# Hybrid decoder step: four buffers for the experts' down weights instead of two, and the last gate rows read at the end

## The reference

```python
scores = sigmoid(xf @ w_router); idx = top 8 of 64 (by groups); w = normalised scores of these * 2.5
def _swiglu(x, wg, wu, wd):              # per expert: wg, wu (1024 x 256), wd (256 x 1024)
    return (silu(x @ wg) * (x @ wu)) @ wd
f = sum over the 8 experts of w * _swiglu(row) + shared expert
x = x + g2 * rms_norm(f, norm_post_ffn)  # g2: the last gate, one row for the prompt, one per sample sequence
```

## Time and profile before

| | us |
|---|---|
| median of 3 runs | 1226.64 (1225.98 to 1227.47) |
| the profiled execution | 1225.67 |
| its span, first to last instruction | 1223.5 |
| TensorE busy | 1106.1 (90%) |
| VectorE busy | 903.4 (74%) |
| ScalarE busy | 642.7 (53%) |
| HBM read and written | 317.00 MB and 42.86 MB |

### The profile page before, as it was taken

How to read it: one execution, slowest core, us unless ns; L and a number is a source line. 1 busy time by engine, 2 the same in 40 slices (tenths; PEclk the granted TensorE clock), 3 DMA queues, 4 the chain that set the end, 5 groups by cost and what they waited for, 6 DMA issues and landing times.

```text
span 1223.5 us, 18540 instructions
## 1 busy us (share of the span) xinstructions
PE 1106.1 (90%) x6014; PEld 811.6 (66%) x6014; DVE 903.4 (74%) x1333; ACT 642.7 (53%) x770; POOL 181.9 (15%) x185
## 2 busy tenths in 40 slices
PE   5999999999989999799999999999999999999700
PEld 3899999865444454467777777777777777777500
DVE  4422443365956777579899999989989888888878
ACT  4332221332421233257787777777777777777501
POOL 1000000000110110112222222222222222221102
PEclk9999999998879999899999999999999999999855
DMA  9542221436974143689999999999999999998996
GB/s 341 188 133 80 80 80 40 157 98 202 315 276 132 44 138 120 235 325 381 380 388 391 391 384 385 387 387 381 373 381 383 373 381 379 375 375 314 352 360 210
DMA packets 86545, 339.34 MB, mean 277 GB/s; under 512 B 12561, under 2 KB 36129, under 8 KB 59122
## 3 DMA queue, kind: packets, MB, share of 16 engines
q1 hardware_dynamic: 70130, 301.16, 67.2%
q0 software_dynamic: 16384, 37.78, 8.8%
HBM read 317.00 MB, written 42.86 MB: 294 GB/s over the span
## 4 chain that ended last, share of the span: by engine, by line
PE 46%; DMA 32%; DVE 14%; ACT 6%; issue 2%; SPq 1%; DVEq 0%; POOL 0%; POOLq 0%; ACTq 0%
DMA arena<-in_w_exp_down 28%; PE ps L1828 11%; DVE down_lo L1648 4%; PE ps L2259 4%; PE ps L2067 4%; ACT down_hi L1120 4%; PE ps L2238 3%; PE ps L2239 3%; PE ps L2240 3%; PE ps L1821 2%; PE ps L2242 1%; PE ps L2105 1%; PE ps L2226 1%; DMA arena<-expert_rows 1%; PE ps L2140 1%
## 5 line engine op out<-in xcount | busy, mean ns | idle before, releaser
L1653 DVE TENSOR_TENSOR gu_lo<-w_gu,gu_hi 128x2048 fp32r<-128x2048 f32 (+1 forms) x128 | 258.7, 2022 | 6.4 <-ACT gu_hi L1114 1.1
L1114 ACT ACTIVATE gu_hi<-w_gu 128x2048 fp32r<-128x2048 f32 (+1 forms) x128 | 217.9, 1703 | 0.0
L1648 DVE TENSOR_TENSOR down_lo<-arena,down_hi 128x2048 fp32r<-128x2048 f32 x64 | 146.7, 2293 | 58.0 <-ACT down_hi L1120 58.0
L2238 PE MATMUL ps<-gu_hi,xT_hi 128*112 128x512 f32 x448 | 182.8, 408 | 3.3 <-DVE xT_lo L1658 2.2
L2239 PE MATMUL ps<-gu_lo,xT_hi 128*112 128x512 f32 x448 | 177.9, 397 | 0.0
L2240 PE MATMUL ps<-gu_hi,xT_lo 128*112 128x512 f32 x448 | 177.3, 396 | 0.0
L1120 ACT ACTIVATE down_hi<-arena 128x2048 fp32r<-128x2048 f32 x64 | 122.7, 1918 | 64.0 <-DMA arena<-in_w_exp_down 56.1
L814 POOL DMA_INDIRECT expert_rows<-arena,row_idx x64 | 69.1, 1079 | 356.2 <-ACT arena L1159 340.1
L2259 PE MATMUL ps<-down_hi,actT_hi 128*112 128x512 f32 x256 | 106.6, 416 | 5.5 <-DVE actT_lo L1643 5.5
L807 POOL DMA_INDIRECT arena<-h_rows,token_idx x64 | 80.6, 1259 | 203.1 <-PE ps L2226 156.1
L1828 PE MATMUL ps<-w_hi,hT_hi 128*128 128x300 f32 x352 | 105.6, 300 | 1.4 <-DVE w_lo L1231 1.4
(11 more groups left out here) (310 smaller groups left out, 1989.8 us busy)
## 6 DMA issues: line engine op xcount, KB each, us to landing
w_gu<-in_w_exp_gate SPq DMA_DIRECT2D x64, 1024.0 KB
w_gu<-in_w_exp_up SPq DMA_DIRECT2D x64, 1024.0 KB
arena<-in_w_exp_down SPq DMA_DIRECT2D x64, 1024.0 KB
arena<-in_w_ada SPq DMA_DIRECT2D x16, 1024.0 KB, 6.9
arena<-in_w_in SPq DMA_DIRECT2D x12, 1200.0 KB, 5.6
arena<-expert_rows SPq DMA_DIRECT2D x9, 1024.0 KB, 13.4
arena<-in_w_ada_first SPq DMA_DIRECT2D x4, 2048.0 KB, 16.2
arena<-expert_rows SPq DMA_DIRECT2D x4, 2048.0 KB, 13.0
```

Source lines behind the costliest of these rows:

```text
L1114: a.activation(gu_hi[b % RING][:, :, ks], w_gu[b % U][:, :, ks], ACT.Copy).then_inc(s_ghi, 1)
L1648: v.tensor_tensor(down_lo[:, :, :], w_dn[b % RING], down_hi[:, :, :].bitcast(F32), ALU.subtract).then_inc(s_dlo, 1)
L1653: v.tensor_tensor(gu_lo[b % U][:, :, ks], w_gu[b % U][:, :, ks], gu_hi[b % RING][:, :, ks].bitcast(F32), ALU.subtract).then_inc(s_glo, 1)
L2238: pe.matmul(out, x_hi, gu_hi[r][:, :, k], start=(k == 0), stop=False)
```

## The change

The raw down weights get four buffers, one per block of a turn, and `load_down` is issued four blocks ahead, right behind `load_gate_up` of the same block. The two new buffers are not contiguous: each row of 8 KB is laid in two pieces of 4 KB, 20 KB apart or more, in gaps of the arena (`apart`). To free these gaps, `x_raw`, `onehot`, `tab`, `bcg2` and a few sums move to other offsets. Down loads of blocks 2 and 3 are now issued ahead of the loop in place of the gate rows, which are read after it: the 0.5 MB read first of all, the eight small ones behind the third `ranks_low` read. No down load is left after the loop. Two semaphores of the front part are used again, with a base of 32 to the count. ScalarE loses one wait (for the x1 store) ahead of its first `x_high`.

```diff
-        x_raw = region(PROJ0 + 4 * D, 2, KT - SPLIT, T)
-        HB0 = XT0 + 4 * SPLIT * T
+        x_raw = region(XT0 + 4 * SPLIT * T, 2, KT - SPLIT, T)
+        HB0 = XT0 + 4 * KT * T
...
-        w_dn = [region(a + W_COLS[0], FK, D) for a in RING_AT]
+        def apart(first, second):
+            return arena[:, first:first + 2 * (second - first)].rearrange("p (k n) -> p k n", k=FK)[:, :, 0:D]
+
+        DN3 = (ARENA_W - 2 * (ARENA_W - WORK0 - 10 * D), WORK0 + 10 * D)
+        w_dn = [region(a + W_COLS[0], FK, D) for a in RING_AT] + [apart(PROJ0 + 4 * D, PROJ0 + 9 * D), apart(*DN3)]
...
-        s_wdn = [sem(f"w_down_in{r}") for r in range(RING)]
+        s_wdn = [sem(f"w_down_in{r}") for r in range(RING)] + [s_cond, s_const]
+        WDN_BASE = (0, 0, 32, 32)
...
-                    sp.wait_ge(s_dlo, j - RING + 1)
+                    sp.wait_ge(s_dlo, j - U + 1)
...
-                sp.dma_start(w_dn[b % RING], down).then_inc(s_wdn[b % RING], 16)
+                sp.dma_start(w_dn[b], down).then_inc(s_wdn[b], 16)
...
             load_gate_up(3, 3, False)
-            sp.dma_start(bcg2[0]...)                       # 0.5 MB
-            for b in range(SB): sp.dma_start(bcg2[1]...)   # 8 x 32 KB
+            load_down(2, 2, False)
+            load_down(3, 3, False)
             last = last_turn(sp)
             with sp.Fori(0, last) as i:
                 for b in range(U):
                     load_gate_up(i * U + (U + b), b, True)
-                    load_down(i * U + (b + RING), (b + RING) % U, True)
+                    load_down(i * U + (U + b), b, True)
...
-            load_down(last * U + RING, RING, True)
+            sp.wait_ge(s_dlo, last * U + 1)
+            sp.dma_start(bcg2[0]...)
             sp.wait_ge(s_free, last * U + 2)
             for t in range(2):
                 sp.wait_ge(s_gu, last * U + (t + 1))
                 rank_rows(ranks_low[t], 0, 4, t)
-            load_down(last * U + 3, 3, True)
             for t in range(2, NT):
...
                 rank_rows(ranks_low[t], 0, 4, t)
+                if t == 2:
+                    for b in range(SB): sp.dma_start(bcg2[1]...)
             sp.wait_ge(s_gu, last * U + 4)
+            sp.wait_ge(s_dlo, last * U + 3)
             for rows, buf in kept(N, shared): ...
             sp.wait_ge(s_free, last * U + 4)
-            sp.wait_ge(s_dlo, last * U + 3)
...  (ScalarE)
-                a.wait_ge(s_wdn[b % RING], 16 * (turns * 2 + (b % U // RING - 1)))
+                a.wait_ge(s_wdn[b % U], WDN_BASE[b % U] + 16 * turns)
...
-            a.wait_ge(s_mst, 32 + 32)
             x_high(0, 0)
```

More of the change, by code:

```diff
@@ L106 @@
 W_COLS = (2 * KT * FF, FK * D)
+GU_HI0, GU_HI1 = WORK0 + W_COLS[0] + W_COLS[1], HT0 + D // 2
+assert GU_HI0 + 2 * KT * FF == WORK0 + 10 * D and GU_HI1 + 2 * KT * FF <= ST0
 def _constants():
@@ L202, in hybrid_step @@
         actT_lo = over_arena("actT_lo", MOD0 + 2 * FK * D + 2 * FK * T, [P, 2, FK, T])
-        gu_hi = [over_arena(f"gu_hi{n}", at, [P, 2, SPLIT, FF]) for n, at in enumerate((WORK0 + W_COLS[0] + W_COLS[1], HT0))]
+        gu_hi = [over_arena(f"gu_hi{n}", at, [P, 2, SPLIT, FF]) for n, at in enumerate((GU_HI0, GU_HI1))]
         gu_lo = [over_arena(f"gu_lo{n}", at, [P, 2, KT, FF]) for n, at in enumerate(GU_AT)]
@@ L207, in hybrid_step @@
         pos_tab = over_arena("pos_tab", POS0, [P, MAXC * ECOL * NT], BF16)
-        OH0 = POS0 + MAXC * ECOL * NT // 2
+        OH0 = _consts["selp"][0]
+        TAB0 = _consts["chunk"][0] + 10 - 4 * P
         onehot = over_arena("onehot", OH0, [P, 2, NT, T], BF16)
-        XT0 = (OH0 + NT * T + 15) // 16 * 16
+        assert OH0 + NT * T <= TAB0 and TAB0 >= _consts["before"][0] + P and TAB0 + 4 * P <= _consts["dret"][0]
+        XT0 = (POS0 + MAXC * ECOL * NT // 2 + 15) // 16 * 16
         xT_hi = over_arena("xT_hi", XT0, [P, 2, SPLIT, T])
@@ L332, in hybrid_step @@
         rowf = small(5, P, rows=1)
-        tab = region(_consts["before"][0] + P, 4, P, rows=1).bitcast(I32)
+        tab = region(TAB0, 4, P, rows=1).bitcast(I32)
         act_rows = region(MOD0 + 2 * FK * D + 4 * FK * T, 2, FF)
         silu_g = region(MOD0 + 2 * FK * D + 4 * FK * T + 2 * FF, 2, FF)
-        w_dn = [region(a + W_COLS[0], FK, D) for a in RING_AT]
+        def apart(first, second):
+            return arena[:, first:first + 2 * (second - first)].rearrange("p (k n) -> p k n", k=FK)[:, :, 0:D]
+        DN3 = (ARENA_W - 2 * (ARENA_W - WORK0 - 10 * D), WORK0 + 10 * D)
+        w_dn = [region(a + W_COLS[0], FK, D) for a in RING_AT] + [apart(PROJ0 + 4 * D, PROJ0 + 9 * D), apart(*DN3)]
+        assert DN3[0] >= HB0 + 2 * D and DN3[0] + D <= WORK0 and DN3[1] + D == GU_HI1
         x_rows = region(HB0, 2, D)
@@ L353, in hybrid_step @@
         ranks_low = [region(GU_AT[t % 3 if t < 3 else t - 3], 4, D) for t in range(NT)]
-        ranks_mid = [region(a, 2, D) for a in (ST0 + D, WORK0 + D, WORK0 + W_COLS[0] + W_COLS[1], HT0, WORK0 + W_COLS[0])]
+        ranks_mid = [region(a, 2, D) for a in (ST0 + D, WORK0 + D, GU_HI0, GU_HI1, GU_HI1 + 2 * D)]
         ranks_high = [region(a, 2, D) for a in (ST0 + W_COLS[0], MOD0, MOD0 + 2 * D, _consts["dret"][0], HB0)]
-        ffn_sum = [region(a, D) for a in (HB0 + 2 * D, POS0, _consts["dret_s"][0], WORK0, ST0)]
-        assert HB0 + 3 * D <= WORK0 and POS0 + D <= XT0
+        ffn_sum = [region(a, D) for a in (WORK0 + W_COLS[0], POS0, _consts["dret_s"][0], WORK0, ST0)]
+        assert MAXC * ECOL * NT // 2 <= D
         sq2 = region(WORK0 + 8 * D, D)
-        bcg2 = [region(WORK0 + W_COLS[0] + W_COLS[1] + 2 * SPLIT * FF, D), region(HT0 + 2 * SPLIT * FF, D)]
-        assert WORK0 + W_COLS[0] + W_COLS[1] + 2 * SPLIT * FF + D <= HT0 and HT0 + 2 * SPLIT * FF + D <= ST0
+        bcg2 = [region(WORK0 + W_COLS[0] + D, D), region(GU_HI0 + 3 * D, D)]
         ps = ctx.enter_context(nc.psum_tensor("ps", [P, 8, 512], F32))
         xT_ps = ps[:, 4:6, :].rearrange("p b (q n) -> p (b q) n", n=XQ)[:, :, 0:T]
-        s_const = sem("consts_in")
-        s_cond = sem("cond_in")
+        s_const = sem("consts_and_fourth_down_in")
+        s_cond = sem("cond_and_third_down_in")
         s_rows = sem("rows_first_sample_rows_and_gla_state_in")
@@ L728, in rank_rows @@
                 sp.dma_start(to[0:ROWS[t], 0:k], by_rank[t * P:t * P + ROWS[t], first:first + k]).then_inc(s_yb[t], 16)
-            load_down(last * U + RING, RING, True)
+            sp.wait_ge(s_dlo, last * U + 1)
+            sp.dma_start(bcg2[0].rearrange("p (c n) -> p c n", n=512), mod_row[1, 0:1, 2:4].broadcast_to([P, 2, 512])).then_inc(s_bcg, 16)
             sp.wait_ge(s_free, last * U + 2)
@@ L741, in _ @@
                 rank_rows(ranks_low[t], 0, 4, t)
+                if t == 2:
+                    for b in range(SB):
+                        sp.dma_start(bcg2[1][b * SS:(b + 1) * SS].rearrange("p (c n) -> p c n", n=512),
+                                     mod_row[1, 1 + b:2 + b, 2:4].broadcast_to([SS, 2, 512])).then_inc(s_bcg, 16)
             sp.wait_ge(s_gu, last * U + 4)
+            sp.wait_ge(s_dlo, last * U + 3)
             for rows, buf in kept(N, shared):
@@ L1116, in down_high @@
             def down_high(j, b, turns):
-                a.wait_ge(s_wdn[b % RING], 16 * (turns * 2 + (b % U // RING - 1)))
+                a.wait_ge(s_wdn[b % U], WDN_BASE[b % U] + 16 * turns)
                 if not (isinstance(j, int) and j < 1):
                     a.wait_ge(s_y, j)
-                a.activation(down_hi[:, :, :], w_dn[b % RING], ACT.Copy).then_inc(s_dhi, 1)
+                a.activation(down_hi[:, :, :], w_dn[b % U], ACT.Copy).then_inc(s_dhi, 1)
             gate_up_high(0, 0, 0, 1)
@@ L1647, in down_low @@
                 v.wait_ge(s_dhi, j + 1)
-                v.tensor_tensor(down_lo[:, :, :], w_dn[b % RING], down_hi[:, :, :].bitcast(F32), ALU.subtract).then_inc(s_dlo, 1)
+                v.tensor_tensor(down_lo[:, :, :], w_dn[b % U], down_hi[:, :, :].bitcast(F32), ALU.subtract).then_inc(s_dlo, 1)
             def gate_up_low(j, b, part):
```

## The result

The changed kernel is slower: 1238.43 us, median of 9 runs (1228.65 to 1240.38), against 1226.64 for the kernel before in the same comparison (9 runs). The ratio is 1.009, 95% interval 1.0063 to 1.0116. A second comparison gave 1236.23 against 1226.06, ratio 1.0105 (1.0072 to 1.0138). The forecast of 1227.1 and its range up to 1231.0 are both missed. The profiled execution took 1236.46 us, its span is 1234.3.

A forecast was written before the change was run, and what follows sets the result against it. The prediction took one lagging DMA engine to bound the stage up to the landing of the shared rows, VectorE after it. Terms 0 - 0.6 - 1.0 + 2.1 = +0.5 us gave 1227.1, no change; range 1221.5 to 1231.0.

The forecast's parts named there:

- Gate rows: Nine gate-row reads moved from ahead of the loop to its end: -0.6 us, bounds -2.4 and +2.4.
- Rival D: Eight small reads at the end hold up third to fifth rank reads by 2.4 to 4 us: 1230.1, chance 0.11.
- The laggard: One DMA engine far behind the rest, with work queued from about 545 to about 1134, taken as true bound.
- Waits of the down loads: In the loop, down-load waits vanish, TensorE regains 5 us, gate/up has an estimated 6 us slack; worth 0 at the end.
- Two down loads to the front: Two down loads of 2.7 us each, added ahead of the loop and taken from the end, cancel: 0.
- The gap at the first rank read: After the last load, about 1 us with little moving closes because block 59's scatter comes earlier: -1.0 us, bounds 0 and -1.6.
- Rows in two pieces: 4 KB pieces in the new down buffers make 32 of 64 down loads 2.4% slower: +2.1 us on the DMA stream.
- Rival A: The whole loop gain reaches the end, as no last engine is the bound: about -5.5 us, 1221.1, chance 0.16.
- B: Rival: gate rows nearly free at the end, with the gap closed and pieces costing 1: -3.0 us, 1223.6, chance 0.12.

## Why the prediction was wrong

**The step that failed** is *Gate rows*: "At the end the same nine reads stand in the same kind of queue, so I cost their move at nothing but this 0.6". Measured for that move alone: +7.5 us (4.5 to 10.3); within the changed kernel the eight small reads are worth 11.9. The upper bound, +2.4, was three to five times too small: I took it from the bytes and the rate of the front, where loads behind the small reads have buffers in hand. The two queues are of another kind. At the end of the loop the last part of a down load landed 7 to 9 us behind the fifteenth in both kernels, and the time did not follow the waits for loads (50.5 us of ScalarE before, 17.3 after, over 560 to 1120). At the end each rank read from the fourth on is issued only when VectorE has freed its buffer or finished a sum, and VectorE waits for the last part: a late part delays a sum, which delays the next issue, so that less is queued (292 GB/s in 1160 to 1190, 345 before). Lateness that the loop absorbs is paid there. Rival D named the right reads and the right side, at 0.11, with 3.5 us from the same bound where 7.5 to 11.9 were measured. My text said that VectorE's last 44 us should be unchanged; the loss was already ahead of them and in them. Nor does VectorE pass the landing of the shared rows on one to one: it came 5.9 us later (1179.9 for 1173.9), the end 10.8; the rest are waits for reads behind it.

**The laggard.** The premise held in part. An engine is last at the end of the loads (0.05 and 0.07). The landing events of the changed kernel show how it gets there: the last part of a down load was 0.1 us or less behind the fifteenth up to 655, then 2.9 us at 696, 5.7 at 897 and 8.8 at 1098; the kernel before has 2.0 at 695 and 7.6 at 1132. And the loop's rate is fixed: with the down waits gone, or with 25 us of gate/up waits, the time is the same. But a late engine isn't a property of the stream that goes on to the end: in the kernel before, the parts land together from the first rank read on (within 0.6 us there), and in the changed kernel without the small reads from the fifth.

**Waits of the down loads.** Right that they go and that gate/up is late next. Wrong in size: I gave gate/up 6 us of slack and let TensorE keep its 5 us; it kept none (560 to 1120: 556.78 us busy, before 557.59). A load landed 27 us after its issue, not 20. That TensorE's end is worth nothing was right.

**Two down loads to the front: 0.** Consistent: four buffers with small reads in front give 0.9986.

**The gap at the first rank read, -1.0.** Wrong: the shares are 0.05 and 0.07 where they were 0.06 and 0.37. It was tied to TensorE being 4 to 5 us earlier, which it was not; the first rank read went out 1.5 us earlier.

**Rows in two pieces, +2.1.** Not contradicted: twice as many pieces cost 1.8 us (-1.0 to 4.7), where this price gives 4.2. The interval holds that, and it holds no cost at all as well. The prediction set beside it the Trainium skill, "DMA: Bandwidth & Descriptors", Why small descriptors are slow. Its three cycles per packet beside 64 for 2 KB would make the small reads, 256 KB or 0.7 us at 382 GB/s, an estimated 3.5% dearer than the same bytes in packets of 8 KB. The runs show 7.5 to 11.9 us for their place. So that overhead agrees with the rows, an estimated 2.1 us for the 64 loads, and is far too small for what decided.

**Rival A** fell (the loop gain does not exist), **B** too (the late small reads are not cheap).

## What to carry to other kernels

The price of these DMA reads was not their own but that of what stood behind them: at most about 4 us in front of the loop, 7.5 to 11.9 ahead of the last reads. Ask of each moved transfer whether the next ones have buffers in hand, as in a prefetching loop, or are each waited for and issued on demand, as in a final reduction: there a delay of even one part in sixteen went straight to the end here. And more buffers for one operand of a stream that was already at its rate only handed the wait to the next operand.

## What the runs showed of the hardware

256 KB in 2 KB packets among 1 and 2 MB reads set them back by 7 us, ten times their time at the loop's rate. In the changed kernel they left one of sixteen parts 4 to 8 us late for the next 50 us; with twice as many, seven parts of the fourth read landed about 8 to 9 us after the first eight and one 13. Moved alone into the kernel before they left no single late part, but all parts spread over 3.5 to 9 us. This does not depend on their being eight reads or two, or on shared DRAM rows. At the end the issue of the eight took SP 6.25 us, in front 3.30; it was covered both times. Why 256 KB set the parts back so far is open: which engine serves which packet is not in the trace, and packets of another size in that place were not tried. Moving all nine reads costs 7.5 us in the kernel before and the eight 11.9 in the changed one, but this needs no explanation yet: the ratios to before, 1.0061 (1.0037 to 1.0084) and 1.0105 (1.0072 to 1.0138), overlap, and the tails grow by 14.4 and 13.1 us. DMA's busy share does not show any of this: over 1160 to 1190 it is 1.00 at 292 GB/s and 1.02 at 345.
